# Two gated feed-forward stages: one of three weight subtractions moves from VectorE to GpSimd

## The chip, the cores and the metric

The program runs on one core of a Trainium2 chip. The metric is the device time of one execution in microseconds (us). TensorE is the matmul engine (PE in the profile, with its weight loads in a row of their own, PEld), VectorE is DVE, ScalarE is ACT, GpSimd is POOL, and SyncE (SP) issues most transfers.

## What is computed

The program is two transformer blocks on 256 tokens of width 1024, all in 32-bit floats, in six stages A to F. Stages A and D are the dense feed-forward stages, which the change touches:

```python
def swiglu(x, w_gate, w_up, w_down):
    return (jax.nn.silu(x @ w_gate) * (x @ w_up)) @ w_down
...
    f = swiglu(rms_norm(h, ffn1_pre_norm[l]), ffn1_w_gate[l], ffn1_w_up[l], ffn1_w_down[l])
    h = h + FFN_RESIDUAL_WEIGHT * rms_norm(f, ffn1_post_norm[l])
```

The gate and up weights are 1024 x 2816 each, the down weights 2816 x 1024. Between the two dense stages lie a mixer (stage B) and a cross attention (stage C); behind them a second block with convolution and attention (stage E) and 64 experts (stage F).

## The kernel before

**Tiling.** A dense stage runs over 11 blocks of 256 hidden features (NF). One block brings 3 MB into one of four ring slots (NS): 1 MB of gate, 1 MB of up and 1 MB of down weights. TensorE multiplies numbers of the type fp32r, and each product is made of three: every operand is split into a high part (rounded to fp32r) and a low part (what is left), and high x high, low x high and high x low are added up (PAIRS).

**Cutting the weights.** The split of a block's weights has three pieces of 128x2048 elements: p = 0 and 1 are gate and up for the two halves of the block's features, p = 2 is the down weights. ScalarE writes a piece's high part (`cut` in `act_ff`, line 683) and raises `high_set[p]`. VectorE waits for that, subtracts it from the raw weights (`cut` in `vec_ff`, line 716) and raises `low_set[p]`. Each piece has one buffer pair, `w_high` and `w_low`; the down piece of the last block has a pair of its own, `last_down` (named `last_w_high` and `last_w_low` in the trace). The first block's pieces 0 and 1 are cut ahead, on lines 665 and 672.

**The order of the work.** Step a on TensorE (`pe_ff`): wait for `low_set[0]`, 48 matmuls of gate and up for half 0 of block a, wait for `low_set[1]`, 48 for half 1 (all on line 649), then `second(a - 1)`: wait for the hidden features and `low_set[2]`, 24 matmuls by the down weights of block a - 1 (line 629). Behind the last step comes `second(10)` at once. ScalarE in step a: for each half the Silu (line 697) and then the high part of piece f of block a + 1; then it waits for `down_done`, because `second(a - 1)` has to leave the single buffer, and writes the high part of piece 2 of block a. In the last step it does not wait, since `last_down` is a buffer of its own. VectorE in step a: for each half three small operations on the hidden features (lines 734, 742, 744) and the low part of piece f of block a + 1, and at the end of the step the low part of piece 2 of block a.

```python
            if 1 <= a < n - 1:
                ac.eng.wait_ge(down_done, b)
            cut(a, j, 2)
...
        release.extend((low_set[2], i + 1) for i in range(n))
```

The last line is the second user of `low_set[2]`: it releases the block's ring slot, and SyncE issues the loads of the block four further on when it is raised.

**GpSimd** builds constants, then issues the loads of small parameters and of the gains, one after another in `gain_order` (line 2790); from the third gain on it first waits for `gain_used`, which VectorE raises behind the residual at the end of a stage (line 389). After the last gain it clears a tile (line 1687) and loads the biases with which stage E begins (lines 1688 to 1693). During stages A to D it computes nothing.

Of the kernel before, what the change touches and what calls it, by code (L numbers as in the profile page):

```python
# [19 lines left out]
F32 = mybir.dt.float32  # L20
F32R = mybir.dt.float32r
I32 = mybir.dt.int32
ALU = mybir.AluOpType
# [86 lines left out]
def rounds(eng, n, peel):  # L110


    for a in range(min(peel, n)):
        yield a, 0
    loops = (n - peel) // NS
    if loops > 0:
        with eng.Fori(0, loops) as j:
            for u in range(NS):
                yield peel + u, j
    for a in range(peel + max(loops, 0) * NS, n):  # L120
        yield a, 0
# [7 lines left out]
def program(nc, A, out, ctx):  # L129
# [444 lines left out]
    def raw_piece(s, p):  # L574

        if p == 2:
            return down[s]
        return wide[s].rearrange("p c (k f n) -> p c k f n", k=2, f=2)[:, :, :, p, :]
# [4 lines left out]
    def ff_weight_sems(tag):  # L583

        return [[sem(f"{tag}_{x}{p}") for p in range(3)] for x in ("high_set", "low_set")]
# [120 lines left out]

    def vec_ff(v, tag, n, base, gate_loaded=None):
        _, silu_set, hidden_set, down_done = ff_sems(tag)
        high_set, low_set = ff_weight_sems(tag)
        hidden_step = sem(f"{tag}_hidden_step")  # L710

        def cut(a, j, p):

            v.eng.wait_ge(high_set[p], a + NS * j + 1)
            high, low = last_down if p == 2 and a == n - 1 else ff_w[p]
            v.eng.tensor_tensor(low[:], raw_piece((base + a) % NS, p),  # L716
                                high[:].bitcast(F32), ALU.subtract).then_inc(low_set[p], 1)

        for a, j in rounds(v.eng, n, PEEL):
            b = a + NS * j  # L720
            gated = gate_loaded is not None and a >= 1
            if a >= PEEL:

                v.eng.wait_ge(down_done, b - 1)
            if gated:
                v.eng.wait_ge(gate_loaded[(a - 1) % NS], 16 * ((a - 1) // NS + 1 + j))
            for f in range(2):

                steps = 2 * (2 * b + f) if gate_loaded is None else 3 * (2 * b + f) - 2
                if gate_loaded is not None and a == 0:  # L730
                    steps = 2 * f
                hid, (high, low) = ff_tmp[:, f, :], (x[:, a % 2, f, :] for x in ff_h)
                v.eng.wait_ge(silu_set, 2 * b + f + 1)
                v.eng.tensor_tensor(hid, ff_sg[:, f, :], ps[4 + 2 * (a % 2) + f][:, S:2 * S],
                                    ALU.mult).then_inc(hidden_step, 1)
                if gated:
                    v.eng.wait_ge(hidden_step, steps + 1)
                    v.eng.tensor_tensor(hid, hid, gate_rows[:, (a - 1) % NS, :],
                                        ALU.mult).then_inc(hidden_step, 1)
                    steps = steps + 1  # L740
                v.eng.wait_ge(hidden_step, steps + 1)
                v.eng.tensor_copy(high, hid).then_inc(hidden_step, 1)
                v.eng.wait_ge(hidden_step, steps + 2)
                v.eng.tensor_tensor(low, hid, high.bitcast(F32), ALU.subtract)\
                 .then_inc(hidden_set, 1)
                if a + 1 < n:
                    cut(a + 1, j, f)
            cut(a, j, 2)
        v.eng.wait_ge(down_done, n)

# [3 lines left out]
    def dense(tag, gain_at, first):  # L756
        base = []
        down_done = ff_sems(tag)[3]

        def pe_part(pe):  # L760
            base.append(pe.block)
            pe_tiles_to_features(pe, strided(xn), DC)
            pe_ff(pe, tag, NF)

        def vec_part(v):
            if first:
                v.ask()
                v.ask()
            vec_norm(v, h)
            if first:  # L770
                vec_cut_first(v, tag, base[0], 0)
            vec_cut_x(v, preg[:, gain_at])
            if first:
                vec_cut_first(v, tag, base[0], 1)
            vec_ff(v, tag, NF, base[0])
            vec_residual(v, ff_bank)

        def act_part(a):
            a.root_table()
            act_norm(a, h)  # L780
            if first:
                act_cut_first(a, tag, base[0], 0)
            act_cut_x(a, preg[:, gain_at])
            if first:
                act_cut_first(a, tag, base[0], 1)
            act_ff(a, tag, NF, base[0])
            a.root_table()
            a.eng.wait_ge(down_done, NF)
            act_bank_norm(a, ff_bank, 0.5, BY_TILE)

        if not first:
            cut_ahead["act"] = lambda a: [act_cut_first(a, tag, base[0], p) for p in range(2)]
            cut_ahead["vec"] = lambda v: [vec_cut_first(v, tag, base[0], p) for p in range(2)]

        def sp_part(sp):
            wg, wu = (weight(f"{tag}_w_{x}").rearrange("(p c) n -> p c n", c=DC)
                      for x in ("gate", "up"))
            wd = weight(f"{tag}_w_down").rearrange("(i f p) n -> i p f n", f=2, p=P)
            for i in range(NF):
                at = slice(i * FB, (i + 1) * FB)  # L800
                sp.load(lambda s: [(wide[s][:, :, 0:FB], wg[:, :, at]),
                                   (wide[s][:, :, FB:2 * FB], wu[:, :, at]),
                                   (down[s], wd[i])])
        return pe_part, vec_part, act_part, sp_part


    params = [(preg[:, i], A[n][0].rearrange("(p c) -> p c", c=DC)) for i, n in enumerate(
# [4 lines left out]
        "ffn1_post_norm", "mix_post_norm", "mem_post_norm", "ffn2_post_norm", "norm1_g_2",  # L812
        "norm2_g_2")) if s in STAGES]

    STAGE_PARTS = {"A": dense("ffn1", 0, True), "D": dense("ffn2", 4, False)}

# [1924 lines left out]
    @block.gpsimd  # L2743
    def _(eng):
        g = Steps(eng, g_step)

        def select(ap, pattern, base, mult, op, fill):
            g(eng.affine_select(out=ap, in_=ap, pattern=pattern, compare_op=op, fill=fill,
                                base=base, channel_multiplier=mult))

        half = slice(0, P // 2)
        rest = slice(P // 2, P)
        g(eng.memset(eps[:], EPS))
        g(eng.memset(eps4[:], 4 * EPS))
        g(eng.memset(group_heads[:], 0.0))
        for k in range(GROUPS4):
            g(eng.memset(group_heads[32 * k:32 * k + 1], 1.0))
        g(eng.memset(ident[:], 0.0))
        select(ident[:], [[-1, P]], 0, 1, ALU.not_equal, 1.0)
        eng.sem_inc(consts, 1)  # L2760
        g(eng.memset(tri1[:], 1.0))
        select(tri, [[1, P]], 0, -1, ALU.is_ge, 0.0)
        g(eng.memset(tri_chunk[:], 1.0))
        select(tri_chunk[:], [[1, P]], 0, -1, ALU.is_ge, 0.0)
        g(eng.memset(tri_chunk[half, rest], 0.0))
        g(eng.memset(ones_chunk[:], 0.0))
        g(eng.memset(ones_chunk[half, half], 1.0))
        g(eng.memset(ones_chunk[rest, rest], 1.0))
        g(eng.memset(causal[:], 0.0))
        select(causal[:], [[-1, P]], 0, 1, ALU.is_ge, NEG)  # L2770
        g(eng.memset(causal_chunk[:], 0.0))
        select(causal_chunk[:], [[1, P]], 0, -1, ALU.is_ge, NEG)
        g(eng.memset(causal_chunk[half, rest], NEG))
        g(eng.memset(earlier[:], 1.0))
        select(earlier[:], [[1, 8], [-1, 8]], 0, 0, ALU.is_gt, 0.0)
        g(eng.memset(levels[:], 0.0))
        for k in range(LEVELS):
            w = 1 << k
            part = levels[:, k, :].rearrange("p (i c) -> p i c", c=2 * w)[:, :, w:2 * w]
            g(eng.memset(part, 1.0))  # L2780

            select(part, [[-2 * w, P // (2 * w)], [0, w]], 0, 1, ALU.is_ge, 0.0)
            select(part, [[2 * w, P // (2 * w)], [0, w]], w, -1, ALU.is_gt, 0.0)
        eng.sem_inc(consts, 1)
        for dst, src in params[PRE_GAINS:]:
            eng.dma_start(dst, src, allow_slow_non_contiguous=True).then_inc(params_loaded, 16)
        for k, name in enumerate(gain_order):
            if k >= 2:
                eng.wait_ge(gain_used, k - 1)
            eng.dma_start(gainb[k % 2][:], A[name][0].partition_broadcast(P))\  # L2790
               .then_inc(gain_loaded[k % 2], 16)
        if "E" in STAGES:
            pool_E(eng, g, gain_order.index("norm1_g_2"))
        if "F" in STAGES:
            pool_F(eng, g, "E" not in STAGES)
# [24 lines left out]
```

## Time and profile before

| | us |
|---|---|
| median of 3 runs | 1860.84 (1858.53 to 1864.0) |
| profiled execution, its own time | 1856.41 |
| its span in the profile | 1854.4 |
| TensorE matmul busy | 1635.6 (88%) |
| VectorE busy | 762.9 (41%) |
| ScalarE busy | 390.2 (21%) |
| GpSimd busy | 29.7 (2%) |

The span runs from the first to the last instruction that the profiler saw; the time of the execution has about 2 us more around it. Stage A lies at about 9 to 220 us of the span, stage D at about 662 to 870 us. TensorE's weight loads and matmuls overlap, so a step of the matmul work is best timed from the start of one group to the start of the next.

### The profile page before, as it was taken

What the parts mean: (1) busy time and instruction counts of PE and PEld (TensorE: products, weight loads), DVE (VectorE), ACT (ScalarE), POOL (GpSimd) and SP (SyncE); (2) the same over time, 40 slices, a digit from 0 to 9 for tenths busy, and PEclk for the clock granted to TensorE, in tenths of its full rate; (3) what the DMA queues carried; (4) which work ended last, traced back from release to release, by engine and by line L of the source; (5) the groups of instructions that cost most, each with busy time, mean ns of one, the idle gap of its engine ahead of it and who ended that gap; (6) DMA issues with size and microseconds to landing.
All of it is one profiled execution on the core that took longest, in us unless ns stands there. A gap on an engine that the chain in (4) does not pass through costs nothing.

```text
span 1854.4 us, 25688 instructions
## 1 busy us (share of the span) xinstructions
PE 1635.6 (88%) x10138; PEld 1078.9 (58%) x10138; DVE 762.9 (41%) x1290; ACT 390.2 (21%) x617; POOL 29.7 (2%) x76
## 2 busy tenths in 40 slices
PE   6999799548799789997899997988899899999896
PEld 6999686548577569995764454435334334344342
DVE  4555404667421355554399755244112112121112
ACT  4333310310010233332101253011111111111110
POOL 4000000000000000001000000000000000000000
PEclk9999899779899889998899988988999999999998
DMA  9653344100244245546244352274687786887885
GB/s 333 203 199 115 106 154 138 46 1 1 89 150 159 69 163 189 204 158 229 103 172 146 136 187 86 91 256 181 262 322 261 292 333 215 315 318 288 343 350 222
DMA packets 138767, 351.62 MB, mean 190 GB/s; under 512 B 9503, under 2 KB 54559, under 8 KB 124320
## 3 DMA queue, kind: packets, MB, share of 16 engines
q1 hardware_dynamic: 135728, 342.97, 50.4%
q0 software_dynamic: 1632, 3.98, 0.7%
q10 hardware_dynamic: 1296, 3.17, 0.4%
q8 instruction: 72, 1.18, 0.3%
q14 instruction: 39, 0.32, 0.0%
HBM read 580.78 MB, written 2.10 MB: 314 GB/s over the span
## 4 chain that ended last, share of the span: by engine, by line
PE 38%; DMA 11%; DVE 9%; SPq 4%; issue 2%; ACT 1%; POOL 0%; DVEq 0%; ACTq 0%
DMA ring<-in_w_exp_gu 9%; PE bank L649 7%; PE bank L1727 6%; PE bank L2438 6%; DVE arena L1928 5%; PE bank L2464 4%; PE bank L629 3%; PE bank L2370 2%; PE bank L2349 2%; SPq L2658 2%; SPq L2667 2%; PE bank L1718 2%; PE bank L469 1%; DMA ring<-in_w_exp_down 1%; SPq L2672 1%
## 5 line engine op out<-in xcount | busy, mean ns | idle before, releaser
L649 PE MATMUL bank<-x_high,w_high 128*128 128x256 f32 x704 | 201.2, 286 | 5.8 <-DVEq L248 5.8
L649 PE MATMUL bank<-x_low,w_high 128*128 128x256 f32 x704 | 200.8, 285 | 0.0
L649 PE MATMUL bank<-x_high,w_low 128*128 128x256 f32 x704 | 199.9, 284 | 0.0
L1727 PE MATMUL bank<-ring,xT 128*128 128x512 f32 x384 | 167.9, 598 | 3.3 <-DVEq L2032 2.1
L716 DVE TENSOR_TENSOR w_low<-ring,w_high 128x2048 fp32r<-128x2048 f32 x60 | 137.4, 2292 | 75.4 <-ACT w_high L683 75.1
L2438 PE MATMUL bank<-ring,xT 128*32 128x512 f32 x1024 | 123.4, 632 | 27.2 <-DMA ring<-in_w_exp_gu 27.2
L649 PEld LDWEIGHTS bank<-x_high,w_high 128*128 128x128 f32 x704 | 134.3, 191 | 7.2 <-issue 6.5
L649 PEld LDWEIGHTS bank<-x_high,w_low 128*128 128x128 f32 x704 | 135.6, 193 | 0.0
L2438 PE MATMUL bank<-ring,xn 128*32 128x512 f32 x1024 | 119.7, 615 | 17.5 <-DMA ring<-in_w_exp_gu 17.5
L649 PEld LDWEIGHTS bank<-x_low,w_high 128*128 128x128 f32 x704 | 134.5, 191 | 0.7
L1727 PEld LDWEIGHTS bank<-ring,xT 128*128 128x128 f32 x384 | 73.2, 192 | 95.2 <-issue 92.8
L683 ACT ACTIVATE w_high<-ring 128x2048 fp32r<-128x2048 f32 x60 | 114.5, 1912 | 59.2 <-PE bank L629 59.2
L2464 PE MATMUL bank<-ring,arena 128*32 128x512 f32 x1024 | 118.0, 601 | 6.3 <-DMA ring<-in_w_exp_down 5.6
L2593 DVE SCALAR_TENSOR_TENSOR arena<-bank,arena 128x256 f32<-128x256 f32 x32 | 15.5, 484 | 259.0 <-ACT arena L2637 259.0
L2438 PEld LDWEIGHTS bank<-ring,xT 128*32 128x32 f32 x1024 | 34.8, 116 | 113.7 <-issue 91.3
L483 PE MATMUL bank<-xT,ring 128*128 128x256 f32 x448 | 99.3, 385 | 0.0
L1928 DVE SCALAR_TENSOR_TENSOR arena<-arena,sm 128x256 f32<-128x256 f32 x240 | 95.2, 476 | 0.0
L483 PEld LDWEIGHTS bank<-xT,ring 128*128 128x128 f32 x448 | 86.6, 193 | 12.6 <-issue 0.5
L2438 PEld LDWEIGHTS bank<-ring,xn 128*32 128x32 f32 x1024 | 34.2, 113 | 99.8 <-issue 78.2
L2603 DVE TENSOR_TENSOR y_low<-bank,y_high 128x512 fp32r<-128x512 f32 x64 | 44.3, 692 | 107.5 <-ACT y_high L2643 107.5
L2464 PEld LDWEIGHTS bank<-ring,arena 128*32 128x32 f32 x1024 | 30.4, 110 | 69.4 <-issue 59.4
L2349 PE MATMUL bank<-picks,tokens_high 128*128 128x256 f32 x256 | 69.2, 304 | 0.0
(512 smaller groups left out, 2251.0 us busy)
## 6 DMA issues: line engine op xcount, KB each, us to landing
ring<-in_w_exp_gu SPq DMA_DIRECT2D x256, 1024.0 KB
ring<-in_w_exp_down SPq DMA_DIRECT2D x128, 1024.0 KB
ring<-in_w_in SPq DMA_DIRECT2D x42, 768.0 KB, 5.7
ring<-in_ffn_w_gate SPq DMA_DIRECT2D x22, 1024.0 KB, 5.5
ring<-in_ffn_w_up SPq DMA_DIRECT2D x22, 1024.0 KB, 8.0
ring<-in_ffn_w_down SPq DMA_DIRECT2D x22, 1024.0 KB, 10.4
ring<-in_w_ada SPq DMA_DIRECT2D x24, 768.0 KB, 6.1
ring<-in_w_in SPq DMA_DIRECT2D x21, 512.0 KB, 6.6
```

The costliest lines, as they stand in the source:

```text
L483: ins = pe.eng.matmul(ps[b][:, k * S:(k + 1) * S], w[:, c, (f + k) * P:(f + k + 1) * P], rhs[:, c, :], start=c == 0, stop=c == DC - 1)
L629: ins = pe.eng.matmul(ff_bank(t, m)[:], ff_h[x][:, a % 2, f, t * P:(t + 1) * P], (last_down if last else ff_w[2])[w][:, f, m * 512:(m + 1) ...
L649: ins = pe.eng.matmul(bank[:, k * S:(k + 1) * S], ff_w[f][w][:, c, k, :], (x_high, x_low)[x][:, c, :], start=c == 0 and i == 0, stop=c == ...
L683: ac.eng.activation(high[:], raw_piece(s, p), ACT.Copy).then_inc(high_set[p], 1)
L716: v.eng.tensor_tensor(low[:], raw_piece((base + a) % NS, p), high[:].bitcast(F32), ALU.subtract).then_inc(low_set[p], 1)
L1718: ins = mm(ps[b][:, k * S:(k + 1) * S], w[:, c, (f + k) * P:(f + k + 1) * P], xT[:, c, :], start=c == 0, stop=c == DC - 1)
L1727: ins = mm(ps[b][:], lhs[:, c, t * P:(t + 1) * P], w[:, c, :], start=c == 0, stop=c == DC - 1 and bias is None)
L1928: ins = stt(acc[:, c, :], src, taps[:, c, i:i + 1], acc[:, c, :], ALU.mult, ALU.add)
L2349: ins = mm(bank[:, n * 256:(n + 1) * 256], part[:, t, c, :], picks[q % 2][:, t].rearrange("p m s -> p (m s)"), start=t == 0 and x == 0, st ...
L2438: ins = mm(ps[4 + half][SEATS * g:SEATS * (g + 1), :], packed[q % 2][:, c, at:at + SEATS], wide[s][:, c, :], start=c == 0, stop=c == DC - ...
L2464: ins = mm(ps[6 + n][r, :], hidT[:, j, r], down[s][:, j, n * 512:(n + 1) * 512], start=j == 0, stop=j == 1, skip_group_check=True)
L2603: do(tt(y_low[:, n, :], ps[6 + n][:], y_high[:, n, :].bitcast(F32), ALU.subtract), y_low_set)
```

## The change

The subtraction of piece 2 is taken out of `vec_ff`. A new function for GpSimd, `pool_ff`, has it for all 11 blocks of a dense stage, in the same buffers and behind the same semaphore `high_set[2]`, and raises the same `low_set[2]`. GpSimd calls it for stage A behind the issue of its second gain, and for stage D behind the issue of its fifth.

```diff
                 if a + 1 < n:
                     cut(a + 1, j, f)
-            cut(a, j, 2)
         v.eng.wait_ge(down_done, n)
+
+    def pool_ff(eng, tag, n, base):
+        high_set, low_set = ff_weight_sems(tag)
+        for a, j in rounds(eng, n, PEEL):
+            eng.wait_ge(high_set[2], a + NS * j + 1)
+            high, low = last_down if a == n - 1 else ff_w[2]
+            eng.tensor_tensor(low[:], raw_piece((base + a) % NS, 2), high[:].bitcast(F32),
+                              ALU.subtract).then_inc(low_set[2], 1)
...
-        return pe_part, vec_part, act_part, sp_part
+        return (pe_part, vec_part, act_part, sp_part), \
+            lambda eng: pool_ff(eng, tag, NF, base[0])
...
-    STAGE_PARTS = {"A": dense("ffn1", 0, True), "D": dense("ffn2", 4, False)}
+    STAGE_PARTS, POOL_FF = {}, {}
+    for x, how in (("A", ("ffn1", 0, True)), ("D", ("ffn2", 4, False))):
+        STAGE_PARTS[x], POOL_FF[x] = dense(*how)
...
             eng.dma_start(gainb[k % 2][:], A[name][0].partition_broadcast(P))\
                .then_inc(gain_loaded[k % 2], 16)
+            if k in (1, 4):
+                POOL_FF["A" if k == 1 else "D"](eng)
```

On VectorE, in the first two steps of stage A, which are written out ahead of the loop (lines 734 to 744 are the hidden features, line 716 the low part of a piece of weights), the order was and is:

```order
-L716 TENSOR_TENSOR w_low<-ring,w_high 128x2048 x2
-L734 TENSOR_TENSOR arena<-arena,bank 128x256
-L742 CAST hidden_high<-arena 128x256
-L744 TENSOR_TENSOR hidden_low<-arena,hidden_high 128x256
-L716 TENSOR_TENSOR w_low<-ring,w_high 128x2048
-L734 TENSOR_TENSOR arena<-arena,bank 128x256
-L742 CAST hidden_high<-arena 128x256
-L744 TENSOR_TENSOR hidden_low<-arena,hidden_high 128x256
-L716 TENSOR_TENSOR w_low<-ring,w_high 128x2048 x2
+L716 TENSOR_TENSOR w_low<-ring,w_high 128x2048
+L734 TENSOR_TENSOR arena<-arena,bank 128x256
+L742 CAST hidden_high<-arena 128x256
```

The second of the two pieces that stood in a row at a step's end (x2) is gone; a step now ends with one.

On GpSimd the changed kernel has this, from the two gains issued at the start (now line 2800) to the third one behind stage A; line 755 is the subtraction, and what lies between the two lines 117 is a loop that runs twice:

```order
56 L2800 DMA gainb<-in_mix_post_norm 128x1024
57 L755 TENSOR_TENSOR w_low<-ring,w_high 128x2048 x2
58 L117 UNCONDITIONAL_BRANCH
59 L117 ISA
60 L755 TENSOR_TENSOR w_low<-ring,w_high 128x2048
...
66 L755 TENSOR_TENSOR w_low<-ring,w_high 128x2048
67 L117 REGISTER_ALU
68 L117 COMPARE_AND_BRANCH
69 L755 TENSOR_TENSOR last_w_low<-ring,last_w_high 128x2048
70 L2800 DMA gainb<-in_mem_post_norm 128x1024
```

Two pieces, eight in the loop and the last block's piece have come between two gain loads that stood next to each other.

## Rows read from the trace of the kernel before

**Rows 1.** The page, engines: busy us, share of the span, instructions.
```profile
PE 1635.6 (88%) x10138; PEld 1078.9 (58%) x10138; DVE 762.9 (41%) x1290; ACT 390.2 (21%) x617; POOL 29.7 (2%) x76
```

**Rows 2.** A window within stage A: length, busy per engine, granted clock, DMA share, GB/s.
```profile
50.00:100.00 50.00, 50.00 (x357) 47.25 (x356) 26.50 (x28) 18.90 (x15) 0.00 (x0) 1.00 0.64 217
```

**Rows 3.** The page's groups: count, busy us, mean ns, idle time before.
```profile
L716 DVE TENSOR_TENSOR w_low<-ring,w_high 128x2048 fp32r<-128x2048 f32 x60 | 137.4, 2292 | 75.4 <-ACT w_high L683 75.1
```

**Rows 4.** Timelines, stage A, one middle step: start us, us, engine, instruction.
```profile
53.91 2.29 DVE L716 TENSOR_TENSOR w_low<-ring,w_high 128x2048 fp32r<-128x2048 f32 x1 [2.88 <-ACT w_high L683]
58.23 0.42 DVE L734 TENSOR_TENSOR arena<-arena,bank 128x256 f32<-128x256 f32 x1 [2.03 <-ACT arena L697]
51.96 1.92 ACT L683 ACTIVATE w_high<-ring 128x2048 fp32r<-128x2048 f32 x1 [3.26 <-PE bank L629]
63.17 0.30 PEld L629 LDWEIGHTS bank<-w_high,hidden_high 128*128 128x128 f32 x2
```

**Rows 5.** Timelines, the first down piece, stage A.
```profile
35.27 3.71 ACT L683 ACTIVATE w_high<-ring 128x2048 fp32r<-128x2048 f32 x2
46.19 0.31 PEld L629 LDWEIGHTS bank<-w_high,hidden_high 128*128 128x128 f32 x2
```

**Rows 6.** Timelines, the last down piece, stage A.
```profile
199.81 1.91 ACT L683 ACTIVATE last_w_high<-ring 128x2048 fp32r<-128x2048 f32 x1
201.76 2.29 DVE L716 TENSOR_TENSOR last_w_low<-ring,last_w_high 128x2048 fp32r<-128x2048 f32 x1 [0.60 <-ACT last_w_high L683]
204.59 0.41 PEld L629 LDWEIGHTS bank<-last_w_high,hidden_high 128*128 128x128 f32 x2
```

**Rows 7.** Timelines, the last down piece, stage D.
```profile
849.54 1.91 ACT L683 ACTIVATE last_w_high<-ring 128x2048 fp32r<-128x2048 f32 x1
854.32 0.41 PEld L629 LDWEIGHTS bank<-last_w_high,hidden_high 128*128 128x128 f32 x2
```

**Rows 8.** Groups on GpSimd by form: count, busy us, mean ns.
```profile
L2748 POOL TENSOR_SCALAR_AFFINE_SELECT levels<-levels 128x64 f32<-128x64 f32 x12 | 5.6, 466 | 0.8
L1687 POOL MEMSET arena<- 128x1024 f32 x1 | 1.0, 970 | 0.0
L2748 POOL TENSOR_SCALAR_AFFINE_SELECT tri<-tri 128x128 f32<-128x128 f32 x1 | 0.3, 293 | 0.1
```

**Rows 9.** Chain of waits behind stage D: start us, us, what.
```profile
868.78 0.28 issue
869.07 0.53 POOL gainb L2790
...
871.37 5.78 DMA arena<-in_b_pw
```

**Rows 10.** TensorE's timeline: pauses and the group behind each; a wait in brackets.
```profile
220.66 3.65 PE L443 MATMUL bank<-ident,xn 128*128 128x128 f32 x16 [10.24 <-DVEq L248]
1039.56 27.70 PE L1727 MATMUL bank<-ring,xT 128*128 128x512 f32 x64 [1.22 <-ACT arena L2079]
1196.49 15.70 PE L1727 MATMUL bank<-ring,xT 128*128 128x512 f32 x32 [2.12 <-DVEq L2032]
1352.83 3.64 PE L2438 MATMUL bank<-ring,xT 128*32 128x512 f32 x32 [2.23 <-DMA ring<-in_w_exp_gu]
1385.07 3.64 PE L2438 MATMUL bank<-ring,xn 128*32 128x512 f32 x32 [1.94 <-DMA ring<-in_w_exp_gu]
1585.26 5.34 PE L2438 MATMUL bank<-ring,xn 128*32 128x512 f32 x32 [2.00 <-DMA ring<-in_w_exp_gu]
1777.48 5.34 PE L2438 MATMUL bank<-ring,xn 128*32 128x512 f32 x32 [2.30 <-DMA ring<-in_w_exp_gu]
```

**Rows 11.** TensorE's window behind the pause at 1196 us: length, busy, granted clock.
```profile
1198.00:1200.00 2.00, 2.00 (x3) 0.50 0.00 0
```

**Rows 12.** Timelines across the end of stage D: SyncE's issues, TensorE's first group of stage E.
```profile
842.01 13.22 SPq L535 DMA_DIRECT2D ring<-in_w_ada  x6
860.08 7.07 PE L1533 MATMUL bank<-ring,cT 128*32 128x512 f32 x64
```

## The prediction

> **What bounds the kernel now.** I read the engines' busy times first: TensorE is busy 88% of the span, VectorE 41%, GpSimd 2% [rows 1]. That is an average, so I went to a window inside a dense stage. There TensorE has matmuls in all 50 us at the full granted clock (1.00, that is 2.4 GHz), VectorE is busy about half, and the DMA share is 0.64 [rows 2]. The dense stages are bound by TensorE; to take work from VectorE gains time only where TensorE waits for VectorE. The group of the subtractions shows where VectorE's own idle time comes from: 75.1 of 75.4 us before them is waiting for ScalarE's high part [rows 3]. So a low part begins as soon as its high part is there, and the question is how long each of them may take before TensorE misses it. That is read at three places.
>
> **A middle step.** ScalarE ends the down piece's high part at 51.96 + 1.92 = 53.88, VectorE's low part follows at 53.91, and TensorE takes the first down weights of that block at 63.17 [rows 4]. From high part to need are 9.3 us, of which 2.3 are used.
>
> **The first block.** Two high parts end at 35.27 + 3.71 = 38.98; the need is at 46.19 [rows 5]: 7.2 us.
>
> **The last block.** Here the order differs: `second(10)` comes directly behind `second(9)`, with no gate and up matmuls between. The high part ends at 199.81 + 1.91 = 201.72, VectorE's low part lasts from 201.76 to 204.05, and TensorE wants it at 204.59 [rows 6]: 2.87 us, of which 2.3 are used, so half a microsecond is spare. In stage D the same: 849.54 + 1.91 = 851.45, need at 854.32, 2.87 us [rows 7].
>
> **The change part by part.**
>
> *Removed:* 22 pieces of 2.29 us on VectorE [rows 3], 50 us of busy time. None of it lies on the path: it is hidden by TensorE's matmuls, and by rows 6 even the last piece ended before its need. Worth nothing in time.
>
> *Added:* 22 pieces on GpSimd. Call one T. The trace has no two-input operation on GpSimd, so T is bounded [rows 8]. Below: a memset of 1024 elements takes 0.97 us, and work that also reads can't be faster, so 2048 take at least 1.9 us. Above: the selections on the 64-element level masks take 466 ns on average, 7.3 ns an element, which gives 14.9 us. Between them stands the nearest row by form, a dense selection on 128x128 that reads and writes: 293 ns, 2.3 ns an element, hence 4.7 us for 2048. It has a fixed part that I don't subtract, since it reads one tensor and this reads two. I take **T = 4.7 us**. The Trainium skill ("GPSIMD Engine Reference", Performance versus the Vector engine) gives 4497 ns for a 2048-element fp32 tensor_tensor, against 2293 ns on VectorE; the latter agrees with the 2292 ns of rows 3, no row here shows the former. By 4.5 each pause below would be 0.2 us shorter.
>
> *Middle steps and first blocks:* 4.7 us, with about 0.1 us for GpSimd to see the semaphore, fits into 9.3 and 7.2 us. Cost nothing; the cover is TensorE's 96 gate and up matmuls, and it is gone for T above 9.1 and 7.0 us.
>
> *Last blocks:* the low part is ready T + 0.2 us behind the high part (0.1 us each for GpSimd and TensorE to see their semaphores; between the 0.04 us of VectorE in rows 6 and the 0.28 us of GpSimd behind stage D in rows 9). TensorE pauses T + 0.2 - 2.87 = **2.03 us**, in each dense stage. What is queued behind the waiting matmuls is the whole of the stage's end: the norm on ScalarE, the residual on VectorE, and then the next stage. Behind stage A TensorE stands idle 10.24 us for exactly this chain, up to 220.66 [rows 10]; behind stage D it runs from `gain_used` over GpSimd's issues to the bias transfer of 5.78 us [rows 9]. Nothing later absorbs it. Twice 2.03 is **+4.1 us**.
>
> *The ring:* `low_set[2]` also releases the slot, so loads are issued T - 2.3, about 2.4 us, later. The tightest is the fourth block of w_ada, whose transfers are the last three of those that end at 855.23 [rows 12], needed when TensorE is three quarters through its group of 7.07 us from 860.08, at 865.4. That leaves 10 us, against 5.78 us from issue to landing for the bias transfer of rows 9, and TensorE itself is 2 us later. Nothing. Elsewhere the released slot is read again only four steps on.
>
> *GpSimd's queue:* the third and the sixth gain now stand behind the subtractions. They wait for a residual that comes later than `second(10)`, hence later than the last piece. Nothing.
>
> *The clock:* a pause of 2 us in a run of full matmuls is new here, and rows show that such pauses sometimes lower the clock. Behind 1.22 us the next 64 large matmuls take 27.70 us, 433 ns each; behind 2.12 us, 32 of them take 15.70 us instead of 13.85, which is 1.85 us more [rows 10], and the window behind shows 0.50 granted, 1.2 GHz [rows 11]. In the expert stage groups of 32 take 3.64 us behind pauses of 2.23 and 1.94 us, and 5.34 us behind 2.00 and 2.30 us, 1.7 more. Of these five pauses near 2 us three cost about 1.8 us and two nothing. So the clock costs nothing, 1.8 or 3.6 us for the two pauses together; with 3 in 5 for each, one fall is likeliest.
>
> **Sum.** 4.1 + 1.8 = **+5.9 us** on the profiled execution (1856.41 to about 1862.3), which is 0.32%. The median of the runs shown is 4.4 us above that execution, so I set the same step on it: 1860.84 + 5.9 = **1866.7 us**. About 0.3%, or 5.6 us, is what a measurement of this kernel can tell from no change, and the sum falls right on that edge.
>
> **The rivals.** The forecast itself, T near 4.7 us and one fall of the clock, has a chance of 0.28; what comes out below the edge by a smaller T is counted with rival 1.
>
> 1. *The clock holds in both stages, or GpSimd is at the skill's 4.5 us with one fall.* +4.1 or +5.5 us, 1865 to 1866.3: within 0.3%. For it: two of five pauses kept the clock; against it: both stages have to be lucky, or T has to be at the lower value. Chance 0.44.
> 2. *Not slower at all.* The point that decides is T = 2.67 us: below it the last piece still meets its need, and the change moves nothing. For it: the memset's rate gives 1.9 us. Against it: a memset reads nothing, and the selection is more than twice as slow. 1860.8, chance 0.04. A gain needs a place where TensorE waits for VectorE's piece, and rows 6 show the last one done 0.5 us early; I leave 0.02 to chance.
> 3. *The clock falls in both.* 4.1 + 3.6 = +7.7 us, 1868.5. Chance 0.17.
> 4. *GpSimd is slow, or the two engines hold each other up.* At twice my T, 9.4 us, each last block costs 6.7 us, each first one 2.4, and the 18 middle steps 0.3: about +24 us. At 14.9 us the middle steps cost 14.9 + 0.2 - 9.3 = 5.8 us each, 104 us for these alone, and TensorE would be bound by GpSimd. For it: GpSimd's slow selections; against it: these have short inner rows, the piece is dense. For the holding up: with T = 4.7 a middle piece runs from 53.98 to 58.7 and meets only VectorE's product at 58.23 [rows 4]; at the last block VectorE has nothing to do. Chance 0.05. The Trainium skill ("SBUF — State Buffer", the section on ports) has VectorE operations with two SBUF inputs and GpSimd reads exclude each other. By it the first piece of stage A waits for VectorE's last cut, half a microsecond, and the sum stays.
>
> **How the numbers follow.** Slower by over 0.3%: the forecast, rival 3 and rival 4, 0.28 + 0.17 + 0.05 = 0.50. Within 0.3%: rival 1 and rival 2, 0.44 + 0.04 = 0.48. Faster: the 0.02 left to chance. The range holds the clock's cases with T from about 3 us (pauses of 0.3 us, +0.7) up to 7 us (2 x 4.3 + 1.8 = +10.4): with the runs' own spread, 1861 to 1872. Left out are most of rivals 2 and 4.
>
> **What would show it.** In the changed profile: VectorE busy near 713 us; GpSimd near 133; 22 GpSimd pieces of one duration near 4.7 us; TensorE without idle time in the middle steps; one pause of about 2 us ahead of the first matmul on `last_w_high` in each dense stage; VectorE's groups otherwise of the same mean. A last group of 24 matmuls that takes over 7 us instead of 5.5 would be the clock. The prediction is wrong if no such pause is there, if TensorE waits for `w_low` in the middle steps, or if the stages behind take back the delay.

## The result and the profile after

The change costs 0.3%: 1866.32 us median of 9 runs (1861.29 to 1872.35) against 1860.84 us (9 runs, 1856.44 to 1864.0) of before, a ratio of 1.0032 with a 95% interval of 1.0017 to 1.0047. That is +6.0 us, between +3.2 and +8.7. A second set of 11 runs of the same kernel (below, e5) gave 1.0038 (1.0022 to 1.0055). The interval of the first set lies wholly above 1, so the kernel is slower, by an amount close to the smallest that such runs can show.

The profiled execution took 1863.23 us, its span is 1861.5. The page's row of engines, against [rows 1]:

```profile
PE 1638.8 (88%) x10138; PEld 1081.9 (58%) x10138; DVE 717.4 (39%) x1268; ACT 390.3 (21%) x617; POOL 131.3 (7%) x98
```

VectorE lost 45.5 us and GpSimd gained 101.6. The groups of GpSimd by form (count, busy us, mean ns, idle time before) give the price that was missing in [rows 8]:

```profile
L755 POOL TENSOR_TENSOR w_low<-ring,w_high 128x2048 fp32r<-128x2048 f32 x20 | 92.4, 4622 | 253.5 <-ACT w_high L683 253.5
L755 POOL TENSOR_TENSOR last_w_low<-ring,last_w_high 128x2048 fp32r<-128x2048 f32 x2 | 9.1, 4572 | 14.4 <-ACT last_w_high L683 14.4
```

One piece takes 4.6 us, twice VectorE's 2.29 (the median of the first group is 4588 ns; one piece in each stage takes 4.9, see below). In the middle of stage A nothing has moved on TensorE. The window of [rows 2] again (length, busy per engine, granted clock, DMA share, GB/s):

```profile
50.00:100.00 50.00, 50.00 (x357) 47.21 (x357) 19.85 (x24) 18.89 (x15) 13.77 (x3) 1.00 0.62 209
```

The end of stage A is where it shows. Timelines of ScalarE, GpSimd, TensorE's weight loads and its matmuls, against [rows 6]:

```profile
198.57 1.91 ACT L683 ACTIVATE last_w_high<-ring 128x2048 fp32r<-128x2048 f32 x1
200.56 4.57 POOL L755 TENSOR_TENSOR last_w_low<-ring,last_w_high 128x2048 fp32r<-128x2048 f32 x1 [7.20 <-ACT last_w_high L683]
205.24 0.30 PEld L629 LDWEIGHTS bank<-last_w_high,hidden_high 128*128 128x128 f32 x2 [1.93 <-issue]
205.28 0.70 PE L629 MATMUL bank<-last_w_high,hidden_high 128*128 128x512 f32 x2 [1.54 <-POOL last_w_low L755]
```

The high part ends at 198.57 + 1.91 = 200.48, GpSimd starts 0.08 us later and ends at 205.13, and the first weights of `second(10)` are loaded 0.11 us behind that. From the end of the high part to these weights it was 2.87 us before and is 4.76 now: a delay of 1.89 us, called the pause below. The matmuls themselves, whose rows have the idle time in brackets, stood idle for 1.54 us. Stage D has the same within 0.02 us (855.16, 859.93). By the end of the group of 24 matmuls 1.80 us of it are left in each stage, **3.6 us** in all. The waits of all engines show the same two and no other wait of TensorE for a GpSimd piece:

```profile
PE bank L629 <- POOL last_w_low L755: 3.1, 2, 1.5
```

The clock did not fall there. TensorE's windows over the pause and the first matmuls behind it (length, busy, granted clock, DMA share, GB/s) have 1.00 throughout:

```profile
202.00:204.00 2.00, 1.73 (x8) 1.00 0.00 0
204.00:206.00 2.00, 0.72 (x3) 1.00 0.00 0
206.00:208.00 2.00, 2.00 (x10) 1.00 0.80 256
```

So the forecast total came out while one of its terms was not where it had been put. Over single executions the span differs by some microseconds anyway (the nine runs spread over 11 us), so the difference of the two spans can't be read as the cost of the change. The experiments had to say whether all 22 pieces or only the last ones cost, and what the clock adds.

### The profile page after: what moved, and what is told of

It is laid out like the page before. It is cut to its first block, busy times and chain, and to the rows that moved or that the text cites. A ratio compares the mean times of both kernels' runs of the same rounds, so it can differ in the third digit from the quotient of the medians.

```text
span 1861.5 us, 25710 instructions
## 1 busy us (share of the span) xinstructions
PE 1638.8 (88%) x10138; PEld 1081.9 (58%) x10138; DVE 717.4 (39%) x1268; ACT 390.3 (21%) x617; POOL 131.3 (7%) x98
## 4 chain that ended last, share of the span: by engine, by line
PE 39%; DMA 10%; DVE 9%; SPq 4%; issue 2%; ACT 1%; POOL 0%; DVEq 0%; ACTq 0%
DMA ring<-in_w_exp_gu 8%; PE bank L649 7%; PE bank L2448 6%; PE bank L1737 6%; DVE arena L1938 5%; PE bank L2474 4%; PE bank L629 3%; PE bank L2380 2%; PE bank L2359 2%; SPq L2668 2%; SPq L2677 2%; PE bank L1728 2%; PE bank L469 1%; DMA ring<-in_w_exp_down 1%; SPq L2682 1%
## 5 line engine op out<-in xcount | busy, mean ns | idle before, releaser
L755 POOL TENSOR_TENSOR w_low<-ring,w_high 128x2048 fp32r<-128x2048 f32 x20 | 92.4, 4622 | 253.5 <-ACT w_high L683 253.5
L716 DVE TENSOR_TENSOR w_low<-ring,w_high 128x2048 fp32r<-128x2048 f32 x40 | 91.7, 2292 | 22.6 <-ACT w_high L683 22.6
L734 DVE TENSOR_TENSOR arena<-arena,bank 128x256 f32<-128x256 f32 x44 | 18.6, 422 | 177.8 <-ACT arena L697 177.7
```

Source lines behind the costliest of these rows:

```text
L716: v.eng.tensor_tensor(low[:], raw_piece((base + a) % NS, p), high[:].bitcast(F32), ALU.subtract).then_inc(low_set[p], 1)
L755: eng.tensor_tensor(low[:], raw_piece((base + a) % NS, 2), high[:].bitcast(F32), ALU.subtract).then_inc(low_set[2], 1)
```

## The experiments

All ratios are against the kernel before, run on the same chip beside them, with a 95% interval in brackets. The profile of each gives one execution.

### Where the cost is

**e1: the last piece back on VectorE**, the other ten of each stage on GpSimd. The last piece gets a semaphore of its own, since two engines would raise one otherwise.

```diff
+            if a == n - 1:
+                cut(a, j, 2)
         v.eng.wait_ge(down_done, n)
...
         for a, j in rounds(eng, n, PEEL):
+            if a == n - 1:
+                continue
```

> GpSimd subtracts the down pieces of blocks 0 to 9, VectorE that of the last block as before (with a semaphore of its own). Theory: the whole cost lies in the last piece; TensorE's pause ahead of last_w_high is gone in both dense stages, the 20 GpSimd pieces near 4.6 us stay hidden, and the time is that of before within 1.5 us (1859 to 1862). Rival: the middle pieces or the contention between VectorE and GpSimd cost something; then the time stays 2 us or more above before.

Measured: 1.0009 (0.9997 to 1.0021), 1860.85 us against 1859.23. The timelines of VectorE and of the weight loads are those of before, high part to need 203.50 - (198.72 + 1.91) = 2.87 us:

```profile
200.66 2.29 DVE L717 TENSOR_TENSOR last_w_low<-ring,last_w_high 128x2048 fp32r<-128x2048 f32 x1 [0.60 <-ACT last_w_high L684]
203.50 0.42 PEld L629 LDWEIGHTS bank<-last_w_high,hidden_high 128*128 128x128 f32 x2
```

**e2: the complement**, only the last piece on GpSimd, again with a semaphore of its own.

```diff
+            if a != n - 1:
+                cut(a, j, 2)
...
-        for a, j in rounds(eng, n, PEEL):
+        for a, j in ((n - 1, 0),):
```

> The complement: VectorE subtracts the down pieces of blocks 0 to 9, GpSimd only that of the last block. Theory: the pause of 1.9 us in each dense stage is there, 3.8 us, and where the granted clock falls behind it some 1.8 us more; 1863 to 1868, the same as with all 22 pieces moved. Rival: a cost of the other 20 pieces; then this is clearly faster than the change.

Measured: 1.0039 (1.0022 to 1.0055), 1865.46 us. Two pieces of 22 cost as much as all of them; the other twenty (e1) cost nothing that can be told from zero, at most 0.21% by its interval.

**e4: the last high part earlier.** The change as it is, with one part of ScalarE's order altered.

```diff
                     cut(a + 1, j, f)
+                elif f == 0:
+                    ac.eng.wait_ge(ff_weight_sems(tag)[1][1], n)
+                    cut(a, j, 2)
             if 1 <= a < n - 1:
                 ac.eng.wait_ge(down_done, b)
-            cut(a, j, 2)
+            if more:
+                cut(a, j, 2)
```

> The change, with ScalarE writing the last block's high down part behind the Silu of half 0 and not of half 1, 5.7 us earlier. Theory: GpSimd's 4.57 us then fit ahead of the need (8.6 us), no pause, the time of before within 1.5 us (1859 to 1862), VectorE 45 us less busy. Rival: moving the work to GpSimd costs by itself, whatever its place; then it stays at 1863 or above.

Measured: 1.0005 (0.9994 to 1.0016), 1859.79 us against 1859.23. Timelines of ScalarE, GpSimd and the weight loads:

```profile
193.18 1.91 ACT L683 ACTIVATE last_w_high<-ring 128x2048 fp32r<-128x2048 f32 x1
195.16 4.60 POOL L759 TENSOR_TENSOR last_w_low<-ring,last_w_high 128x2048 fp32r<-128x2048 f32 x1 [1.44 <-ACT last_w_high L683]
203.72 0.41 PEld L629 LDWEIGHTS bank<-last_w_high,hidden_high 128*128 128x128 f32 x2
```

The same 4.6 us on the same engine now end 4.0 us early. GpSimd's work costs nothing by itself; what costs is a piece of twice the length behind a high part that comes late. No kernel here is faster than before; this one has its time with VectorE 45 us less busy.

### What the clock adds

**e3 and e6: matmuls in the pause.** The same kernel twice, in two sets of runs: 16 matmuls into a bank that nobody reads, ahead of the wait for the last low part.

```diff
+        for _ in range(16):
+            pe.eng.matmul(ps[6][:, 0:S], ff_w[1][0][:, 0, 0, :], x_high[:, 0, :],
+                          start=True, stop=True, skip_group_check=True)
         second(n - 1, 0, False, True)
```

> The change, with 16 matmuls more (128x256, about 1.9 us at full clock) into an unused bank in front of the wait for the last low part, so that TensorE has no pause. Theory of the clock term: the delay of 1.9 us per stage stays (+3.8 us, about 1864.6) but the granted clock never falls in the last group of 24 matmuls, so it is 1 to 2 us faster than the change over many runs and its runs spread less. Rival: the clock term is nothing; then the same as the change. Should the extra matmuls last longer than the pause, it is a little slower.

> The kernel with 16 matmuls in each of the two pauses again, since it came out at 1871.6 us, above the change and not below it. Theory of chance (clock falls elsewhere in the program): this time within 3 us of the change as run beside it. Rival: keeping TensorE busy there costs something itself; then it is again 4 us or more above the change.

Measured: 1.0054 (1.0034 to 1.0073) and 1.0057 (1.0038 to 1.0077), 1871.6 and 1868.8 us; the change beside the second one stood at 1864.72. The idle time is gone, the delay is not: the group of 24 ends 10.62 us behind the high part, 1.92 us later than before. The runs are not faster than the change, as they would be if idle time in that place made the clock fall. The second set, where the change ran beside, puts them 4.1 us above it by the medians; the first set had only e2, with the same two pauses, 6.1 us below. The intervals of the ratios overlap both times (1.0034 to 1.0073 with e2's 1.0022 to 1.0055, 1.0038 to 1.0077 with e5's 1.0022 to 1.0055), so the rival of the second expectation is favoured, not shown. In both profiles stage F is long, 645 us behind its router weights; in the others it lasts 637 to 643, two kernels without these matmuls in stage A (e8, e9) among them with 643. Whether 32 more instructions in stages A and D have to do with it was not found.

**e5: the change again.**

> The change as it is, once more. Theory: 3.8 us of pauses plus the clock term, 1863 to 1868; in its profile two pauses of 1.9 us ahead of the last down group, and if the granted clock falls behind one, that group of 24 matmuls takes over 7 us and not 5.6. Rival: nothing but the pauses costs; then the difference to before, over these and the earlier runs, settles at 3.8 us and no group is longer.

Measured: 1.0038 (1.0022 to 1.0055), 1864.72 us. Two pauses again, and both groups behind them are 5.7 us long. With the first profile, e2 and stage A of e9 (below) these are seven pauses of 1.9 us, each with 1.54 to 1.55 us between matmuls and 5.7 us for the group behind it, and the clock fell behind none:

```profile
205.99 0.70 PE L629 MATMUL bank<-last_w_high,hidden_high 128*128 128x512 f32 x2 [1.54 <-POOL last_w_low L755]
```

**e7: a pause in every step.** GpSimd does each middle piece once, then 800 of its columns, then all of it again.

```diff
+            if 1 <= a < n - 1:
+                for k, cols in enumerate((D, 400)):
+                    eng.tensor_tensor(low[:, :, 0:cols], raw_piece((base + a) % NS, 2)[:, :, 0:cols],
+                                      high[:, :, 0:cols].bitcast(F32), ALU.subtract)\
+                       .then_inc(longer, 1)
+                    eng.wait_ge(longer, 2 * (a + NS * j) - 1 + k)
```

> In the 18 middle steps (9 in each dense stage) GpSimd does the subtraction of the down piece, then 800 of its 2048 columns again, then all of it again: 4.6 + 1.9 + 4.6 + some 0.2 us, about 11.3 us with the waits. By the rule need = 9.3 us behind the high part, each of the 18 steps gets a pause of about 2.1 us, 38 us in all, and the two last pieces their 1.9. If the clock falls behind 3 in 5 of such pauses, at 1.8 us each, 19 us more: about 1922; if it never falls, about 1903. Rival to the budget rule: the middle steps have other slack; then less than 30 us in all. The same profile shows which VectorE instructions grow while GpSimd is at work.

Measured: 1.0377 (1.0349 to 1.0405), 1927.11 us. The waits of TensorE, its timeline behind one pause, and a window of its clock there:

```profile
PE bank L629 <- POOL w_low L762: 33.8, 18, 1.9
```

```profile
85.08 0.70 PE L629 MATMUL bank<-w_high,hidden_high 128*128 128x512 f32 x2 [1.87 <-POOL w_low L762]
85.63 0.62 PE L629 MATMUL bank<-w_high,hidden_low 128*128 128x512 f32 x2
86.09 0.98 PE L629 MATMUL bank<-w_low,hidden_high 128*128 128x512 f32 x2
86.87 1.05 PE L629 MATMUL bank<-w_high,hidden_high 128*128 128x512 f32 x2
...
89.95 0.63 PE L629 MATMUL bank<-w_high,hidden_low 128*128 128x512 f32 x2
```

```profile
87.00:89.00 2.00, 2.00 (x6) 0.50 0.98 340
```

All 18 middle steps wait. A step lasted 17.0 us before and lasts 19.1 us here where the clock held, 20.7 where it fell: the pause is 2.1 us, as the budget of 9.3 us has it, and a fall costs 1.6 us more, 7.15 us for the 24 matmuls and not 5.5. Of the 16 pauses whose group can be timed from start to start, 14 had a fall. The other two, one at the end of each stage, had one too, by the windows behind them:

```profile
230.00:232.00 2.00, 2.00 (x7) 0.50 0.97 364
916.00:918.00 2.00, 2.00 (x7) 0.50 0.82 260
```

The rival to the budget is out. The rows show pairs of matmuls growing from 0.62 to 1.05 us and back, and the window has 0.50, which is 1.2 GHz. One thing expected did not come: TensorE does not wait for the last pieces, since pause and fall had put their need off to 6.6 us behind the high part. Without their 3.8 us, but with 16 falls where 11 were expected, stages A and D account for some 64 us, against 61 expected and about 70 between the medians; the rest was not followed up.

So the size of the clock term was right, but behind pauses of 1.9 us it was paid 0 times in 7, behind 2.1 us in every step 16 times in 18. In the measure of the brackets these are 1.54 us and 1.87 to 1.89 us of idle matmuls. Whether this third of a microsecond or the repetition every 19 to 21 us makes the difference was not tested.

**e8: the kernel before, once more**, for its profile.

> The kernel before, for a second profile. Theory: the stretch from the end of stage A to the end of stage B (302.0 us before, 305 to 309 in the changed kernels) differs from run to run by the granted clock and has nothing to do with the change: here too 303 to 309. Rival: it is 302 again, and the change costs some microseconds in stage B by a way that is not understood.

Its stretch from the end of stage A to the end of stage B is 306.9 us. The first profile of before had 302.0, a short one; this differs from execution to execution without the change. It is one reason why the spans could not be subtracted.

### The other microseconds

Measured by GpSimd's issues, stage D lasts from the fifth gain to the sixth, and stage E from there to the router weights. GpSimd's timeline of the changed kernel:

```profile
669.37 0.95 POOL L2800 DMA_DIRECT2D gainb<-in_norm_g  x1 [143.50 <-DVEq L389]
874.59 0.57 POOL L2800 DMA_DIRECT2D gainb<-in_norm_g  x1 [14.78 <-DVEq L389]
1221.88 0.86 POOL L2304 DMA_DIRECT2D arena<-in_w_router  x1 [341.98 <-DVEq L2075]
```

Stage E is 347.3 us long here and was 345.7, though nothing in it changed. Three more kernels followed this up: e9 is the change with the last piece of stage D on VectorE, so that only stage A pauses; e10 and e11 are the kernel before with 8 and 24 matmuls ahead of `second(10)` in stage D, a plain delay.

```diff
+        for _ in range(8 if tag == "ffn2" else 0):
+            pe.eng.matmul(ps[6][:, 0:S], ff_w[1][0][:, 0, 0, :], x_high[:, 0, :],
+                          start=True, stop=True, skip_group_check=True)
```

> The change, but the last down piece of stage D on VectorE, so that only stage A has the pause of 1.9 us. Theory: stage D, between the ends of stages C and D, is back at 203.5 us from 205.2, and stage E, whose stretch was 347.1 to 347.5 us in the executions with a delay in D and 345.3 to 346.1 in those without, is back at 345.3 to 346.1; over the runs some 2 us above before, 3 to 4 below the change. Rival: stage E's 1.5 us come from the 9 other GpSimd pieces of stage D; then it stays at 347.

> The kernel before with 8 matmuls (128x256, about 0.95 us) ahead of second(10) in stage D, no GpSimd piece and no pause: a plain delay. If stage E's extra 1.5 us come from when its work falls against the changes of the granted clock, its stretch differs from 345.3 to 346.1 by an amount that isn't in proportion to the delay. If a delay costs only itself, stage E is at 345.3 to 346.1 and the time is 1 us above before.

> The same with 24 matmuls, about 2.8 us. Same readings: a delay that costs only itself gives stage E 345.3 to 346.1 and 3 us above before; if any delay in D lengthens stage E, 347 or more here as well; if it is a matter of when the clock changes, it may be either, and differ from the run with 1 us.

The stretches of all these profiles:

| kernel | stage D, us | stage E, us |
|---|---|---|
| before, before again | 203.47, 203.49 | 345.72, 345.29 |
| e9 (pause in A only) | 203.40 | 345.60 |
| e1, e4 (no pause) | 203.69, 203.58 | 345.71, 346.08 |
| e10 (delay of 1 us) | 204.43 | 347.88 |
| the change, e5, e2 (pause) | 205.22, 205.25, 205.28 | 347.29, 347.32, 347.07 |
| e3, e6 (delay, no idle time) | 205.54, 205.50 | 347.49, 347.43 |
| e11 (delay of 3 us) | 206.40 | 346.07 |
| e7 (pauses in every step) | 235.17 | 348.00 |

Stage E is 1.0 to 2.6 us longer for a delay of 1 to 2 us in stage D, whether TensorE idles or not, at most 0.8 longer for 3 us, and some 2.5 longer for the 32 us of e7. It does not follow from GpSimd's other pieces, which e1, e4 and e9 have and do not pay for. What fits is the third reading of the expectations: TensorE idles about 10 us behind stage D at any rate and its clock changes several times there, and the delay decides which matmuls fall into the slow part. The first matmuls of this part of stage E show one such place, in e8 (no delay) and in e5 (pause):

```profile
881.99 1.71 PE L1545 MATMUL bank<-xT,group_heads 128*128 128x512 f32 x2
883.53 1.02 PE L1543 MATMUL bank<-arena,ident 128*128 128x512 f32 x2
```

```profile
886.64 1.92 PE L1555 MATMUL bank<-xT,group_heads 128*128 128x512 f32 x2
888.35 1.47 PE L1553 MATMUL bank<-arena,ident 128*128 128x512 f32 x2
```

The slow part reaches one matmul pair further in e5, and this group of matmuls ends 0.6 us later than in e8, counted from its start. That is a part of the 2.0 us between these two profiles; the rest is inferred from the lengths and one execution each. The timed runs don't confirm it for e10: 0.9997 (0.9988 to 1.0007) leaves no room for the 3.3 us by which its stages D and E are longer. e11 has 1.0008 (0.9994 to 1.0022), e9 1.0008 (0.9991 to 1.0024), where the 1.8 us of one pause lie inside the interval.

### How GpSimd and VectorE hold each other up

At the first block's down piece of stage A the two engines meet. Timelines of VectorE and GpSimd in the changed kernel:

```profile
35.96 2.29 DVE L716 TENSOR_TENSOR w_low<-ring,w_high 128x2048 fp32r<-128x2048 f32 x1 [0.59 <-ACT w_high L683]
39.92 0.42 DVE L734 TENSOR_TENSOR arena<-arena,bank 128x256 f32<-128x256 f32 x1 [1.67 <-ACT arena L697]
40.37 2.50 DVE L742 CAST hidden_high<-arena 128x256 fp32r<-128x256 f32 x1
37.82 4.90 POOL L755 TENSOR_TENSOR w_low<-ring,w_high 128x2048 fp32r<-128x2048 f32 x1 [12.70 <-ACT w_high L683]
```

GpSimd's piece begins while VectorE's cut still runs, to 38.25, and is 0.31 us longer than most others (4.59). VectorE's cast, 0.29 us elsewhere, takes 2.50: it ends at 42.87, just behind GpSimd's piece (42.72). The product on line 734, which reads one operand from PSUM, ran beside the piece at its usual 0.42. In e7, where GpSimd is at work for 11 us of each step, the third kind shows too, line 744 with both inputs in SBUF:

```profile
57.27 0.42 DVE L734 TENSOR_TENSOR arena<-arena,bank 128x256 f32<-128x256 f32 x1 [7.21 <-ACT arena L697]
57.72 2.01 DVE L742 CAST hidden_high<-arena 128x256 fp32r<-128x256 f32 x1
59.77 4.73 DVE L744 TENSOR_TENSOR hidden_low<-arena,hidden_high 128x256 fp32r<-128x256 f32 x1
59.66 4.55 POOL L762 TENSOR_TENSOR w_low<-ring,w_high 128x2048 fp32r<-128x2048 f32 x1
```

It takes 4.73 us instead of 0.43, until GpSimd's piece is over. The Trainium skill ("SBUF — State Buffer", the section on ports) says that a VectorE operation with two SBUF inputs, or in a two-port mode, and a GpSimd operation that reads SBUF shut each other out, and that the one that starts first keeps the ports to its end. These rows agree for lines 742, 744 and 734. In the change this happens twice, once near the start of each stage (2.50 and 2.52 us for the cast), 4.4 us of VectorE's time together. It costs nothing that the runs can tell: e1 and e4 have both of them too, and the time of before within their intervals.

## Why the prediction was right, and where it was not

- **The bound.** TensorE-bound dense stages, nothing to gain from a lighter VectorE: right. The window is full before and after, and e1 and e4, with VectorE 41 to 46 us less busy, are no faster.
- **T.** 4.7 us by the rate of the dense selection; 4.57 measured for the last pieces, which decide, and 4.59 for most others. The Trainium skill's 4497 ns ("GPSIMD Engine Reference", Performance versus the Vector engine) is 0.07 us under the former, the forecast 0.13 over it. The bounds of 1.9 and 14.9 were needed only for the rivals.
- **The budgets.** 9.3, 7.2 and 2.87 us from high part to need. The first block and the middle steps cost nothing measurable (e1), 9.3 us held under test (e7: a pause of 2.1 us, as worked out), and the last block's T - 2.67 gives 1.90 for T = 4.57, where 1.89 was measured. The forecast said 2.03, so +4.1 us for both; 3.6 us arrive at the ends of the groups, because T was 0.1 smaller and 0.1 us comes back at each restart.
- **Busy times.** GpSimd 131 (133 forecast), VectorE 717 (713 forecast); the difference is the two casts that wait.
- **The clock.** This step failed in its place. "Of these five pauses near 2 us three cost about 1.8 us and two nothing" was carried over to the last blocks; there the clock fell in none of seven. The cost of a fall (1.6 us in e7) was well sized, its chance was not. The five pauses came from stages with other work around them, and they were not measured alike: the brackets of [rows 10] give idle time between matmuls, 1.94 to 2.30 us, while the 2.03 us of the forecast is the delay of the weights. In brackets the pause that came is 1.54 us, shorter than each of the five. The chances don't follow from 3 in 5 either: that gives 0.36 for two falls and 0.16 for none, where rival 3 has 0.17 and rival 1, which also holds the lower T, has 0.44.
- **The sum.** +5.9 was forecast, +6.0 measured (+3.2 to +8.7). Of these the delay at the two stage ends, 3.6 us, is shown by rows, and e1, e2 and e4 show that the cost goes and comes with it. The rest stays open. It is probably not nothing: 3.6 us would be a ratio of 1.0019, and e2 and e5 both have 1.0022 as their lower end. Some 1.5 us of it stand in stage E of the profiles, by an effect that was not foreseen, whose cause is inferred and which the timed runs of e10 do not bear out. The agreement to a tenth is luck: the clock term of 1.8 us was not paid where it was put, and microseconds of another, unexplained origin took its place.
- **The rivals.** Rival 1's condition, the clock holding in both stages, came true in every profile of the change; its +4.1 us lies inside the interval of the first set and at the lower end of those of e2 and e5. Of rival 4 the holding up exists, without a price at T = 4.6. That the piece would be short enough for the last block (T under 2.67) was out by nearly 2 us.
- **The ring and GpSimd's queue.** Nothing, as forecast. The group of [rows 12] follows the last down matmuls at once and takes 7.07 us as before. GpSimd issues its third gain at 219.90, 8.92 us behind the end of the last down group (210.98); before it was 219.34 and 210.42, the same 8.92.

```profile
865.60 7.07 PE L1543 MATMUL bank<-ring,cT 128*32 128x512 f32 x64
```

## What to carry to other kernels

Before work moves to a slower idle engine, measure for each kind of step how long its result may take, from what starts it to its first use, and look above all at the last one of a loop, where the work that covered it is no longer there. Here 20 of 22 moves were free within the noise and two carried the cost; starting the last one a half step earlier made them free as well. Differences of a few microseconds in this program can't be read from two spans: compare stretches between fixed events, in several profiles.

## What the runs showed of the hardware

- GpSimd subtracts 128x2048 fp32 elements to fp32r in 4.6 us, VectorE in 2.29 (the change and before).
- While it does, VectorE's cast from SBUF to SBUF and its subtraction with two SBUF inputs wait for its end (from 0.29 to 2.50 us in the change, from 0.43 to 4.73 us in e7), its product with one operand in PSUM does not (0.42).
- The granted clock held at 2.4 GHz behind seven of seven single pauses of 1.9 us at a stage's end (1.54 us between matmuls), and fell to 1.2 GHz behind 16 of 18 pauses of 2.1 us that came in every step (1.87 us between matmuls), each fall costing 1.6 us. Which of the two differences counts was not separated.
- The same work behind stage D took 345.3 to 347.9 us as a delay of 0 to 3 us was put ahead of it, not in proportion to the delay, in one execution of each kernel. This was not expected, and its cause is inferred only.
